# Three stage borders of a one-core transformer kernel: what is loaded first, and on which side of a border rows are scaled and moved

## The reference, cut to what matters

```python
def modulate(x, shift, scale):
    return layer_norm(x) * (1 + scale) + shift
# first block: tokens and context, each with its own shift and scale
mod_x = silu(c) @ ada_w + ada_b ;  mod_c = silu(c_ctx) @ ada_w + ada_b
hc = modulate(ctx, csh1, csc1)
yx = token_mixer(modulate(x, sh1, sc1), p, s_f, s_b)   # z = h @ w_in, then a scan over tokens
x = layer_norm(ALPHA * x + gt1 * yx)
x = layer_norm(ALPHA * x + gt2 * expert_choice_ffn(modulate(x, sh2, sc2)))   # 16 experts
# second block: even layer (differential attention + a linear recurrence), odd layer
# (neighbourhood attention), each on rms_norm(x) * g, scaled by (1 + scale) plus shift
```

## Time and profile before

| | us |
|---|---|
| median of three runs | 3004.95 |
| lowest, highest | 3004.73, 3008.0 |
| profiled execution, first to last instruction (span) | 3007.4 |
| PE busy in it | 2738.7 (91%) |
| DVE, ACT, POOL busy | 1183.6, 608.3, 251.1 |
| first stage | 0 to 47.7 |
| border of experts and even stage | 2327 |
| border of even and odd stage | 2640 |

### The profile page before, as it was taken

One profiled execution on the slowest core, in us unless ns is written; L12 is line 12 of the kernel. 1 busy time (PEld: TensorE's weight loads), 2 busy tenths in 40 slices (PEclk: granted clock), 3 DMA queues, 4 the chain that ended last, 5 costly groups with the idle time before them and its releaser, 6 DMA issues. The chain is left out here.

```text
span 3007.4 us, 69538 instructions
## 1 busy us (share of the span) xinstructions
PE 2738.7 (91%) x31106; PEld 1485.6 (49%) x31106; DVE 1183.6 (39%) x2613; ACT 608.3 (20%) x1255; POOL 251.1 (8%) x282
## 2 busy tenths in 40 slices
PE   5899999999998999988998989989886999899998
PEld 3566666676664444444433433433333455455553
DVE  3564566566643673163221212212003245423333
ACT  3233223333321100000000000000002344322222
POOL 1121122112200000001000000000000021110000
PEclk9999999999999999998999999999998999999999
DMA  6000000000005873166999999999995321042210
GB/s 203 24 26 14 19 25 20 21 19 25 5 33 196 287 273 112 56 267 273 430 431 430 431 430 431 430 430 431 430 430 218 128 77 37 0 122 63 63 42 29
DMA packets 191501, 557.42 MB, mean 185 GB/s; under 512 B 32140, under 2 KB 119714, under 8 KB 166646
## 3 DMA queue, kind: packets, MB, share of 16 engines
q1 hardware_dynamic: 191222, 553.19, 46.9%
HBM read 550.65 MB, written 2.24 MB: 184 GB/s over the span
## 5 line engine op out<-in xcount | busy, mean ns | idle before, releaser
L2320 PE MATMUL bank<-arena,xe 128*64 128x512 f32 x1024 | 347.0, 603 | 35.1 <-DMA gates<-in_exp_w_dram 24.0
L684 PE MATMUL bank<-arena 128*128 128x512 f32 x384 | 201.4, 646 | 6.2 <-DVE vj L1610 5.0
L2320 PEld LDWEIGHTS bank<-arena,xe 128*64 128x64 f32 x1024 | 108.7, 139 | 182.6 <-issue 169.6
L3347 PE MATMUL bank<-arena 128*128 128x512 f32 x384 | 175.8, 606 | 3.4 <-PEq L3225 3.4
L2320 PE MATMUL bank<-arena,hidT 128*64 128x512 f32 x512 | 171.7, 599 | 2.4 <-DMA gates<-in_exp_w_dram 1.9
L2773 PE MATMUL bank<-arena 128*128 128x512 f32 x320 | 142.9, 595 | 0.0
L2320 PE MATMUL bank<-mg_ring,xe 128*64 128x512 f32 x256 | 117.7, 614 | 19.3 <-DMA u<-in_exp_w_dram 19.3
L2320 PE MATMUL bank<-ys,xe 128*64 128x512 f32 x256 | 116.1, 607 | 19.2 <-DMA arena<-in_exp_w_dram 18.5
L2545 DVE TENSOR_TENSOR x<-x,bank 128x512 f32<-128x512 f32 x64 | 43.6, 685 | 227.8 <-PE bank L2358 227.8
L2538 DVE TENSOR_TENSOR hid<-hid,bank 128x512 f32<-128x512 f32 x32 | 19.8, 682 | 285.4 <-PE bank L2320 285.4
L1548 DVE TENSOR_TENSOR pm<-bank,m_level 128x512 f32<-128x512 f32 x120 | 82.7, 689 | 115.7 <-PE bank L763 114.7
(11 more groups left out here) (528 smaller groups left out, 5485.7 us busy)
## 6 DMA issues: line engine op xcount, KB each, us to landing
arena<-in_exp_w_dram SPq DMA_DIRECT2D x96, 2048.0 KB, 26.8
gates<-in_exp_w_dram SPq DMA_DIRECT2D x24, 2048.0 KB, 29.6
ys<-in_exp_w_dram SPq DMA_DIRECT2D x24, 2048.0 KB, 26.1
mg_ring<-in_exp_w_dram SPq DMA_DIRECT2D x24, 2048.0 KB, 25.7
u<-in_exp_w_dram SPq DMA_DIRECT2D x24, 2048.0 KB, 30.2
ws_w<-in_ada_w_dram SPq DMA_DIRECT2D x40, 1024.0 KB, 5.4
arena<-in_odd_w_in_dram SPq DMA_DIRECT2D x32, 512.0 KB, 4.0
arena<-in_w_in_dram SPq DMA_DIRECT2D x24, 512.0 KB, 4.0
```

The lines of the kernel that those rows point to most:

```text
L684: last = mm(to[:], wj[:, c, i, :], hT[:, c, 0:T], start=(c == 0), stop=(c == KT - 1))
L2320: r[e] = mm(out[a, :], lhs[j][:, a], w[:, j, 512 * c:512 * c + 512], start=(first and j == 0), stop=(last and j == len(lhs) - 1), skip_gro ...
L3347: last = mm(o[:], w[:, i, t, :], hT[:, t, :], start=(t == 0), stop=(t == KT - 1))
```

## The change

There are three edits.

1. In the first stage SP loads the tokens first, then the three `c` (now written to `cT[:, i, :]`, contiguous), the context, two chunks of `ada_w`, the eleven small tables, the other two chunks, and the rest as before. The turning of the small tables on PE and their copies on DVE move behind the fourth tile's turn and the sixth tile's norm. The modulation of `hT` leaves the stage; DVE does all eight token blocks and ACT all eight context blocks as the first thing of the scan stage, each raising a counter (`h_x`, `h_c`) on which PE waits block by block.
2. The scaling and moving of the eight turned banks leaves the experts' stage; ACT (even blocks) and DVE (odd) do it first in the even stage, with counters `h_even` and `h_odd` on which PE's first projection waits block by block. PE makes the row after its second projection instead of before the first, and DVE copies it after its small operations.
3. The 21 counters of the odd stage are made in the even stage, where POOL raises them behind its clearing of semaphores; the odd stage's extra block is gone.

```diff
 # stage_modulated_norm, SP
-            with nc.allow_non_contiguous_dma("three small vectors"):
-                for i, c in enumerate((A["c"][0], A["c_ctx"], A["c_2"][0])):
-                    sp.dma_start(cT[:, :, i], c.rearrange("(p j) -> p j", j=KT)).then_inc(S["c_in"], 16)
             sp.dma_start(xt[:, 0:NX, :], A["x"][0].rearrange("(n p) d -> p n d", p=P)).then_inc(S["x_in"], 16)
+            for i, c in enumerate((A["c"][0], A["c_ctx"], A["c_2"][0])):
+                sp.dma_start(cT[:, i, :], c.rearrange("(p j) -> p j", j=KT)).then_inc(S["c_in"], 16)
             sp.dma_start(xt[:, NX:NT, :], A["ctx"][0].rearrange("(n p) d -> p n d", p=P)).then_inc(S["ctx_in"], 16)
+            cond.load(sp, 0)
+            cond.load(sp, 1)
             for dst, src in small:
                 sp.dma_start(dst, src).then_inc(S["rows_in"], 16)
-            for i in chunks:
-                cond.load(sp, i)
+            cond.load(sp, 2)
+            cond.load(sp, 3)
 # its ACT and DVE lists end without the modulation:
-            for j in range(KT):
-                act.activation(hT[:, j, T:TA], hT[:, j, T:TA], ACT.Identity, scale=sc[:, j, 1:2], bias=k.mod[:, j, 1:2]).then_inc(S["moved_c"], 1)
-                if j in X_BY_ACT:
-                    act.activation(hT[:, j, 0:T], ...)
-            for j in range(KT):
-                if j not in X_BY_ACT:
-                    dve.tensor_scalar(hT[:, j, 0:T], hT[:, j, 0:T], sc[:, j, 0:1], k.mod[:, j, 0:1], ALU.mult, ALU.add).then_inc(S["moved_x"], 1)
 # stage_scan, PE in low_rank; ACT and DVE at the head of prologue()
+                    if f == LOW_DECAY:
+                        pe.wait_ge(S["h_c" if context else "h_x"], c + 1)
+                for c in range(KT):
+                    f(hT[:, c, T:TA], hT[:, c, T:TA], ACT.Identity, scale=h_scale[:, c, 1:2], bias=k.mod[:, c, 1:2]).then_inc(S["h_c"], 1)
+                for c in range(KT):
+                    ts(hT[:, c, 0:T], hT[:, c, 0:T], h_scale[:, c, 0:1], k.mod[:, c, 0:1], ALU.mult, ALU.add).then_inc(S["h_x"], 1)
 # stage_experts loses these, stage_even_mixer begins with them (ACT even, DVE odd)
+            for j in range(0, KT, 2):
+                f(hT[:, j, :], bank[j][:], ACT.Identity, scale=k.rms_gain[:, j:j + 1], bias=k.mod[:, 48 + j, 2:3]).then_inc(E["h_even"], 1)
+            for j in range(1, KT, 2):
+                ts(hT[:, j, :], bank[j][:], k.rms_gain[:, j:j + 1], k.mod[:, 48 + j, 2:3], ALU.mult, ALU.add).then_inc(E["h_odd"], 1)
 # stage_even_mixer, PE in project and after the second projection
+                    if turn == 0 and isinstance(t, int) and t == 0:
+                        pe.wait_ge(E["h_odd" if i % 2 else "h_even"], i // 2 + 1)
+                if i == 1:
+                    for h in range(2):
+                        for j in range(4):
+                            last = mm(bank[2 + h][:, j * P:j * P + P], k.mod[:, OUT_ROW + 4 * h + j, 2:3].to_broadcast([P, P]), k.ident[:],
+                                      start=True, stop=True)
+                        last.then_inc(E["row_mm"], 1)
 # stage_even_mixer, POOL behind its clearing of semaphores
+            for n in ODD_COUNTERS:
+                odd_counters[n] = k.sem("na_" + n)
+                pool.sem_inc(odd_counters[n], 1)
 # stage_odd_mixer
-    with nc.Block() as block:
-        @block.sync
-        def _(sp):
-            start_at_one(sp, S)
```

More of the change, by code:

```diff
@@ L354, in _ @@
             normalise(5)
+            dve.wait_ge(S["rows_turned"], 2)
+            own.then(dve.tensor_copy(k.cols1[:], k.bank[ROWS_BANK][:, 0:112]))
+            own.then(dve.tensor_copy(k.cols2[:], k.bank[ROWS_BANK][:, 112:182]))
             own.settle()
@@ L389, in _ @@
             turn(3)
+            pe.wait_ge(S["rows_in"], 16 * len(small))
+            pe.transpose(k.bank[ROWS_BANK][:, 0:112], rows1[:], k.ident[0:112, 0:112]).then_inc(S["rows_turned"], 1)
+            pe.transpose(k.bank[ROWS_BANK][:, 112:182], rows2[:], k.ident[0:70, 0:70]).then_inc(S["rows_turned"], 1)
             cond.product(pe, 2)
@@ L2419, in _ @@
                 for j in range(KT):
[L2420 to L2422 removed]
+                    pe.transpose(bank[j][:, t * P:t * P + P], xn[:, t, j * P:j * P + P], k.ident[:])
         @block.scalar
@@ L2479, in _ @@
             unit_rows(3)
-            for j in range(0, KT, 2):
-                act.wait_ge(S["turned"], j + 1)
-                act.activation(hT[:, j, :], bank[j][:], ACT.Identity, scale=rms_gain[:, j:j + 1],
-                               bias=k.mod[:, 48 + j, 2:3]).then_inc(S["hT_moved_a"], 1)
         @block.vector
@@ L2604, in _ @@
             inverse_root(3)
-            for j in range(1, KT, 2):
-                dve.wait_ge(S["turned"], j + 1)
-                dve.tensor_scalar(hT[:, j, :], bank[j][:], rms_gain[:, j:j + 1], k.mod[:, 48 + j, 2:3],
-                                  ALU.mult, ALU.add).then_inc(S["hT_moved_d"], 1)
 DA_HEADS, LRU_C, LAM_INIT = 4, 8.0, 0.8 - 0.6
@@ L2869, in step @@
                 last.then_inc(S["o_turned"], 1)
-            for h in range(2):
-                for j in range(4):
-                    last = mm(bank[2 + h][:, j * P:j * P + P], k.mod[:, OUT_ROW + 4 * h + j, 2:3].to_broadcast([P, P]), k.ident[:],
-                              start=True, stop=True)
-                last.then_inc(E["row_mm"], 1)
             for i in range(6):
@@ L3028, in _ @@
             tt(rms_gain[:], rms_gain[:], k.cols2[:, 44 + KT:44 + 2 * KT], ALU.mult).then_inc(E["gain_made"], 1)
-            for h in range(2):
-                dve.wait_ge(E["row_mm"], h + 1)
-                dve.tensor_copy(row[:, h, :], bank[2 + h][:]).then_inc(E["row_moved"], 1)
             own.then(dve.memset(eps[:], RMS_EPS))
@@ L3057, in _ @@
             own.last(ts(neglam[:], neglam[:], LAM_INIT, None, ALU.subtract))
+            for h in range(2):
+                dve.wait_ge(E["row_mm"], h + 1)
+                dve.tensor_copy(row[:, h, :], bank[2 + h][:]).then_inc(E["row_moved"], 1)
             dve.wait_ge(S["bias_in"], 1 + 16)
```

59 lines of the change are left out of this document (22 added, 37 removed).

## The result

The changed kernel takes 3013.34 us (median of 20 runs, 3005.14 to 3021.33) against 3007.65 us of the kernel before (20 runs, 3000.43 to 3012.50). The ratio is 1.0021, 95% interval [1.0014, 1.0028]: slower by a fifth of a per cent, where 10 us less were forecast. In the profiled executions the span went from 3007.4 to 3012.4; the execution of after took 3013.96 with a span of 3012.4, so a time is its span and about 1.5 us. On the forecast's own side the sum came to 2995.1 and the range to 2992 to 2999.

What follows compares the result with a forecast made beforehand. PE, busy 2738.7 of 3007.4 us, was taken as the bound, with idle gaps at three stage borders on the path. Gains of 6.8 + 1.0 + 0.45 + 1.6 = 9.85 us off the 3004.95 median gave 2995.1, range 2992 to 2999.

Steps and rivals of the forecast that it cites:

- D: Rival, slower: PE, fed block by block, keeps the low clock through a stage's head; up to 3028.3 us; chance 0.04.
- The order of the loads: First stage: tokens first and contiguous `c` start the load stream earlier, 3.0 us (bounds 0 to 3.7).
- Rival A: The load stream does not start earlier, masks land at 43.1, first border gives 3.8; 2998.1 us; chance 0.07.
- The border: First stage to scan: modulation by blocks, PE starts at 40.95 instead of 47.75, 6.8 us including the earlier loads.
- The clock at the first border: PE's shorter stand of 2.55 us may keep the clock full: 1.0 us gained, from 0.7 lost to 2.8 saved.
- Edit 2: Experts' to even stage: PE starts 0.95 us earlier, 0.5 lost to the clock, 0.45 gained; bounds -0.4 and 0.95.
- Edit 3: Even to odd stage: dropping the extra block gives 1.6 us; clock term taken as 0.
- Rival B: PE starts earlier but full clock returns no earlier than before or later; 6.0 us gained, 2999.0; chance 0.11.
- C: Rival: the clock holds at the first and third border; 14.1 us gained, 2990.9; chance 0.10.

Runs made afterwards that it cites:

- the loads alone: Kernel before with only edit 1's new load order, modulation left in the first stage, all addresses as before: ratio 1.0002 to the kernel before.
- the 32 bytes alone: Kernel before with only a 32-byte tile per partition ahead of later buffers, no instruction changed: 3017.49 us against 3007.11, ratio 1.0034.
- edits 2 and 3 alone: Kernel before with only edits 2 and 3, experts' slots kept at 0 mod 512 by 480 bytes: ratio 0.9997 to the kernel before.
- the 480-byte version: Changed kernel with 480 more bytes behind `rms_gain`, slots again at 0 mod 512: 3001.96 us against 3007.11 for the kernel before, ratio 0.9981.

## Why the prediction was wrong

**The step that failed** is the last sentence of its sum: "the experts' stage, bound by its weights, also starts its loads when slots of the stage before come free, which moves alike". The start did move (3.3 us earlier in the trace of after); the rate behind it was taken as given, with no term for it. The runs showed that 32 bytes of layout lower it from 430 to 427 GB/s, which costs 8.0 us there, more than the three borders give together. The diff had the cause in its first hunk, and the trace had the stage at a flat 430 GB/s, the place where 0.7% of the DMA's rate is the kernel's time. No rival named it: D, the one on the slower side, was about a low clock behind a border, and nothing of it came (one wait for `h_x`, full level back after 5.2 us).

**The order of the loads**: 3.0 forecast, 2.7 in the stream, of which 1.9 reached the masks. With the addresses of before (the loads alone) it is 2.9 in the stream and 2.7 at the masks, so the term was nearly right. What after lacks at the masks is for the most part the same mistake: SP's wait is 8.1 or 8.2 us in the three traces with the arena at 32 or 128 mod 512, also where nothing else was changed, and 7.2 to 7.6 in the ten others that have the masks last (one of them with the arena at 64). `w_low`, the load in front of the masks, lies in the arena, and the masks shift with it; which of the two it is was not tried. Rival A falls. With the chunks at 0 the last one comes at 33.62, another 2.0 earlier than in after; that is rate and no shift of the start, and the forecast had no term for it.

**The border**: PE at 42.85, not 40.95. 1.1 us are the masks. The other 0.8 are the open (0.4 behind SP's wait, 0.3 forecast) and the first block: 0.47 was the mean of six, and the first of eight takes 1.08. It does so in all ten traces with the modulation moved (1.07 to 1.08), and in the four others the first block takes 0.55. In those ten POOL begins the scan stage with a memset of 0.75 us that starts 0.03 or 0.04 before DVE's block; in the four it starts 3 us behind the last of them. The memset of after, then of before:

```profile
41.59 0.75 POOL L1457 MEMSET arena<- 128x780 f32 x1 [32.72 <-POOLq L217]
```

```profile
47.71 0.75 POOL L1464 MEMSET arena<- 128x780 f32 x1 [38.87 <-POOLq L216]
```

So the forecast put the block beside work of POOL that it had not stood beside, and had no term for it. That the memset holds the block up is likely, but no run moved it.

**The clock at the first border**: +1.0 forecast, 0.2 found (5.2 for 5.6 us at half level). "In 36.00:38.00 PE did nothing and the clock stayed full" was true and no ground to hope on: in seven of the fourteen traces here the clock falls at the end of this wait or within the product behind it, which costs the chain up to 1.6 us (5.10 from the last chunk to `sc` with the load order alone, 3.47 in before). Around the border the low stretch was 10.2 us in the profile of before, 6.8 with the 32 bytes alone and 13.7 with edits 2 and 3 alone (there it began in the product), with the same instructions. One profile can't carry a term of 1 us here.

**Edit 2**: 0.95 - 0.5 = 0.45 forecast; 0.84 - 0.5 found. It was right. **Edit 3**: 1.6 forecast at a clock term of 0; 1.47 from the gap, and 1.0 given back. The mechanism was right, and the clock term, which I had bounded by 0.8, was mis-sized. Rival B is so far borne out at the second and third border; C, a clock that holds, at none. What was said to hide the moved work did hide it: PE waits once, and the row copies and POOL's increments delay nothing.

**The sum, without the layout**: the 480-byte version has 5.5 us to K_X and 0.7 at the two later borders, 6.2 in its trace; by the measured ratio, 0.0019 x 3007 = 5.7 [2.1, 9.0]. So even without the 8 us the forecast of 9.85 was too high, by the masks, the first block and the clock; 3001.96 would have been outside the range too.

**What the total can't tell**: stretch two of the table, with the same code in before and in the 32-byte version, took 1329.9 and 1325.4, and over all traces 1318.9 to 1329.9 with the slots at 0 or 256 and 1321.7 to 1331.7 with the others. Between two single profiles 5 us there mean nothing, and whether the layout costs anything in that stretch isn't shown. Each border is to be read at the border, and totals by ratios.

## What to carry over

A new tile, however small, moves every buffer allocated behind it: before any count of instructions, compare the addresses of those buffers that a DMA-bound stage fills, and keep them at multiples of 256 bytes, the fast ones here. Where the engines are full, a step that adds nothing to them still needs a line in the sum, for their rate. And where several tiny terms hang on a clock that falls in short waits, take bounds from several traces, or none.

## What was not expected of the hardware

- DMA writes into SBUF at 32, 64 or 128 mod 256 bytes: 16 KB packets of 611 to 624 ns, in the mean 3.9 to 4.9 more than at 0, and 427 or 428 GB/s in place of 430; the first stage's stream of 2 KB packets 386 to 392 in place of 406. At 0 mod 256 the packets are all but equal: 18306 of 18390 at 611 ns. The misaligned ones split into several values at one address, and why was not tried.
- Behind PE's wait for the last chunk (2.2 to 3.1 us) the clock fell to 1.2 GHz in seven of fourteen traces, mostly when PE was at work again, and stayed full in the other seven, whose waits were as long (2.1 to 2.7). The product takes 1.92 us at full level, up to 3.58 otherwise.
- The first of eight equal modulations takes 1.08 us on DVE, the others 0.53, in all ten traces where a memset of POOL starts just ahead of it, and 0.55 in the four where none does. POOL's second memset of the arena there takes 0.36 us, against 0.12 in before.
